# Output weights of FFN and experts loaded as neighbouring row pairs, with the inner FFN columns taken at a stride of two

## The reference

```python
def swiglu(h, w_in, w_out):
    g, u = jnp.split(h @ w_in, 2, axis=-1)
    return (jax.nn.silu(g) * u) @ w_out
```

## Time and profile before

| | |
|---|---|
| time, median of three runs | 2223.34 us (2221.9 to 2224.48) |
| span of the profiled execution, first to last instruction | 2220.3 us |
| TensorE busy | 2011.6 us, 91% |
| VectorE busy | 1409.2 us, 63% |
| ScalarE busy | 1195.9 us, 54% |
| GpSimd busy | 564.5 us, 25% |
| granted TensorE clock, mean | 0.962 |
| read from memory | 512.10 MB, 231 GB/s over the span |

### The profile page before, as it was taken

One profiled execution on the slowest core, in us unless ns is written; L12 is line 12 of the kernel. 1 busy time (PEld: TensorE's weight loads), 2 busy tenths in 40 slices (PEclk: granted clock), 3 DMA queues, 4 the chain that ended last, 5 costly groups with the idle time before them and its releaser, 6 DMA issues. The chain is left out here.

```text
span 2220.3 us, 25094 instructions
## 1 busy us (share of the span) xinstructions
PE 2011.6 (91%) x8940; PEld 1560.7 (70%) x8941; DVE 1409.2 (63%) x1276; ACT 1195.9 (54%) x1018; POOL 564.5 (25%) x192
## 2 busy tenths in 40 slices
PE   4888779999999788869999999999999999999895
PEld 2556568667678675557877788787877878777784
DVE  5657432544433352457878778787877878787784
ACT  5442442433322334446767676676766767676573
POOL 1310011211210110013324233333333423243232
PEclk9999889999999889989999999999999999999998
DMA  9560212545622221228989899898998979898792
GB/s 347 204 213 20 76 57 95 166 166 179 208 95 72 80 95 39 67 83 306 364 287 365 299 349 356 301 363 295 367 336 312 371 285 361 300 353 324 248 367 85
DMA packets 231745, 513.84 MB, mean 231 GB/s; under 512 B 9129, under 2 KB 34706, under 8 KB 231186
## 3 DMA queue, kind: packets, MB, share of 16 engines
q1 hardware_dynamic: 228498, 507.25, 64.2%
q10 hardware_dynamic: 3200, 5.96, 0.8%
HBM read 512.10 MB, written 1.07 MB: 231 GB/s over the span
## 5 line engine op out<-in xcount | busy, mean ns | idle before, releaser
L170 DVE TENSOR_TENSOR low<-raw,high 128x2048 fp32r<-128x2048 f32 (+2 forms) x484 | 1023.7, 2140 | 404.1 <-ACT high L162 397.3
L162 ACT ACTIVATE high<-raw 128x2048 fp32r<-128x2048 f32 (+1 forms) x484 | 923.7, 1912 | 623.5 <-PE PS L191 491.2
L170 POOL TENSOR_TENSOR low<-raw,high 128x1024 fp32r<-128x1024 f32 x161 | 527.1, 3274 | 1474.0 <-ACT high L162 1474.0
L189 PE MATMUL PS<-high,ah 128*128 128x512 f32 (+1 forms) x1478 | 592.0, 401 | 28.9 <-DVE low L170 12.9
L191 PE MATMUL PS<-high,al 128*128 128x512 f32 (+1 forms) x1478 | 577.5, 391 | 0.0
L190 PE MATMUL PS<-low,ah 128*128 128x512 f32 (+1 forms) x1478 | 577.2, 391 | 0.0
L189 PEld LDWEIGHTS PS<-high,ah 128*128 128x128 f32 x1478 | 280.6, 190 | 112.5 <-POOL low L170 28.0
L191 PEld LDWEIGHTS PS<-high,al 128*128 128x128 f32 x1478 | 280.4, 190 | 58.5
L190 PEld LDWEIGHTS PS<-low,ah 128*128 128x128 f32 x1478 | 281.0, 190 | 53.1
L1769 PE MATMUL PS<-high,ah 128*128 128x512 f32 x504 | 197.7, 392 | 4.0 <-DVE al L1343 4.0
L1771 PE MATMUL PS<-high,al 128*128 128x512 f32 x504 | 197.1, 391 | 0.0
(11 more groups left out here) (251 smaller groups left out, 1372.6 us busy)
## 6 DMA issues: line engine op xcount, KB each, us to landing
raw<-in_moe_w_in_dram SPq DMA_DIRECT2D x252, 1024.0 KB, 7.3
raw<-in_moe_w_out_dram SPq DMA_DIRECT2D x126, 1024.0 KB, 7.5
raw<-in_ada_w_dram SPq DMA_DIRECT2D x48, 1024.0 KB, 6.5
raw<-in_ffn_w_in_dram SPq DMA_DIRECT2D x22, 1024.0 KB, 5.1
raw<-in_ffn_w_out_dram SPq DMA_DIRECT2D x11, 1024.0 KB, 4.8
raw<-in_ab_w_in_dram SPq DMA_DIRECT2D x8, 1024.0 KB, 5.7
raw<-in_ab_w_out_dram SPq DMA_DIRECT2D x4, 1024.0 KB, 6.7
raw<-in_mla_w_o_dram SPq DMA_DIRECT2D x4, 1024.0 KB, 4.9
```

Of the source, the lines that this page charges most:

```text
L162: act.activation(high[n % SPL][:, 0:width], raw[n % RAW][:, 0:width], ACT.Copy).then_inc(high_made, 1)
L170: eng.tensor_tensor(low[n % SPL][:, c0:c1], raw[n % RAW][:, c0:c1], high[n % SPL][:, c0:c1].bitcast(F32), ALU.subtract).then_inc(low_made[ ...
L189: pe.matmul(o, sh, mh, start=start, stop=False)
```

## The change

`ffn_w_out` and `moe_w_out` are viewed by `row_pairs` instead: partition p of a unit holds rows 256u + 2p and 256u + 2p + 1, which lie next to each other in memory. Each partition thus reads one run of 8 KB where it read two runs of 4 KB. The bytes, the number of units and their order stay.

So that the rows of the hidden values match, block j of a pair in `ffn_pair` takes columns j, j+2, j+4, ... of its 256 instead of 128 neighbouring ones, and `turn` takes every second column of 256 of `hh`.

```diff
--- before.py
+++ after.py
@@ -583,8 +583,12 @@
         def rows_of(w):
             return w.rearrange("(k p) n -> p k n", p=P)
 
+        def row_pairs(w):
+
+            return w.rearrange("(u p a) n -> u p a n", p=P, a=2)
+
         abin, about = rows_of(ab_w_in[0]), rows_of(ab_w_out[0])
-        fin, fout = rows_of(ffn_w_in[0]), rows_of(ffn_w_out[0])
+        fin, fout = rows_of(ffn_w_in[0]), row_pairs(ffn_w_out[0])
         wdq, wdkv, wuq, wukv, wo = (rows_of(w[0]) for w in (mla_w_dq, mla_w_dkv, mla_w_uq, mla_w_ukv, mla_w_o))
 
         MLA_W = [4 * CQ] * 2 + [4 * (CKV + CROPE)] * 2 + [1536] * 3 + [2048] * 2 + [2048] * 4
@@ -665,28 +669,28 @@
             for j in range(2):
                 fin_pair(N_FIN + 42 + 2 * j, 0, (9 + j) * 256)
             for j in range(11):
-                load_unit(sp, N_FOUT + j, fout[:, 2 * j:2 * j + 2, :])
+                load_unit(sp, N_FOUT + j, fout[j])
             for j in range(13):
                 load_unit(sp, N_MLA + j, mla_src(j))
 
 
             def visit(v, e):
-                wi, wo_ = rows_of(moe_w_in[0, e]), rows_of(moe_w_out[0, e])
+                wi, wo_ = rows_of(moe_w_in[0, e]), row_pairs(moe_w_out[0, e])
 
                 def up(n, it, col):
                     for j in range(4):
                         load_unit(sp, n + j, wi[:, 4 * (j % 2):4 * (j % 2) + 4, bass.ds(col + (j // 2) * D_FFE, FCH)], it)
 
-                def down(n, it, blk):
+                def down(n, it, pair):
                     for j in range(2):
-                        load_unit(sp, n + j, wo_[:, bass.ds(blk + 2 * j, 2), :], it)
+                        load_unit(sp, n + j, wo_[bass.ds(pair + j, 1)].rearrange("u p a n -> p (u a) n"), it)
 
                 up(U0, v * NCH, 0)
                 with sp.Fori(0, 3) as i:
                     for j in range(2):
                         up(UC + 6 * j, v * NCH + i * 2, i * 1024 + (j + 1) * FCH)
-                        down(UC + 4 + 6 * j, v * NCH + i * 2, i * 8 + j * 4)
-                down(UC + 36, v * NCH, 24)
+                        down(UC + 4 + 6 * j, v * NCH + i * 2, i * 4 + j * 2)
+                down(UC + 36, v * NCH, 12)
 
             with sp.Fori(0, NE) as e:
                 visit(e, e)
@@ -1579,7 +1583,7 @@
                             unit_ready(pe, n + gu, it)
                         if gu == 0 and f >= 2:
                             pe.wait_ge(s["hid_made"], f - 1 + i * 4)
-                        wh, wl = (t[:, :, j * P:(j + 1) * P] for t in halves(n + gu, KD))
+                        wh, wl = (t.rearrange("p k (c a) -> p k c a", a=2)[:, :, :, j] for t in halves(n + gu, KD))
                         for k in range(KD):
                             if f == gu == 0:
                                 low_ready(pe, 1, k)
@@ -1740,7 +1744,8 @@
             def turn(count, par):
                 pe.wait_ge(s["h_made"], count)
                 for j in range(4):
-                    last = pe.transpose(PS[:, 4, j * P:(j + 1) * P], hh[:, par, j * P:(j + 1) * P], ident)
+                    last = pe.transpose(PS[:, 4, j * P:(j + 1) * P],
+                                        hh[:, par, :].rearrange("p (u c a) -> p u c a", c=P, a=2)[:, j // 2, :, j % 2], ident)
                 last.then_inc(s["ht_done"], 1)
 
             def up(n, it, par, parts=(0, 1)):
```

## The result

| | before | after |
|---|---|---|
| median, 11 runs each | 2224.26 us | 2230.6 us |
| ratio of after to before, 95% interval | | 1.003 (1.0018 to 1.0043) |
| span of the profiled execution | 2220.3 us | 2231.6 us |

The change makes the kernel slower by 0.3% (6.3 us between the medians), and the interval leaves no room for no change. The two profiled executions lie further apart, by 11.3 us; the next lines sort out why.

What follows compares the result with a forecast made beforehand. The prediction took TensorE's own instructions as the bound. Transfers, FFN loads and transposes gave 0 + 0 + 0 on a 2220.3 us span; 3.0 us from span to median made 2223.3 us, range 2217 to 2237 us.

Steps and rivals of the forecast that it cites:

- the transposes' bound: Experts' `turn`: 252 transposes with the loads' 53 ns column part doubled and exposed, 13.4 us, total 2237 us; 5 in 100.
- The rival of slower FFN loads: FFN's first product: strided loads cost by their span, up to 68 us, with transposes 81 us, 2305 us; 7 in 100.
- What bounds the kernel: Whole kernel: bound by TensorE's own instructions, busy 91% of the span; no transfer in the loop.
- The transfers, 0: FFN and expert output weights: 137 transfers in 8 KB runs, hidden behind TensorE's work, 3.5 us reserve; 0 us.
- transfers become the bound: Expert stage: 8 KB runs moving 20% slower would add 45 us over 63 chunks, 2268 us; 4 in 100.
- disturb the splits less: Expert stage: half as many runs might shorten GpSimd's splits, some 5 us back, 2218 us; 5 in 100.
- The strided transposes: Experts' `turn`: 252 strided transposes keep loads of 140 ns, taken as 0 us; upper bound 13.4 us.
- The strided loads of the FFN: `ffn_pair`, FFN's first product: 1056 loads at a stride of two floats, taken as 0 us; upper bound 68 us.
- 38 ns of each interval are free: FFN's first product: a load shown with 189 ns leaves 38 ns of the 0.227 us between matmul starts.
- the 0.23 us that was to show the prediction wrong: Sign in the FFN's trace: an interval between matmuls grown past 0.23 us means the prediction is wrong.
- The comparison by bytes per ns: FFN loads: strided span needs 10 bytes per ns, packed transpose loads read 9.7, bf16 some 23; so 0 us.
- The Trainium skill's rule on 16-byte lines: FFN's strided loads: full-rate reads need two accesses per 16-byte line; stride two has exactly two, so 0 us.

Runs made afterwards that it cites:

- e1: Against the kernel before, only `moe_w_out` is loaded in 8 KB runs, with TensorE's reads packed; 2224.59 us, ratio 1.0003.
- e11: Changed kernel, but ScalarE, VectorE and GpSimd sort the FFN's columns in the splits; 48 loads stay strided; 2221.86 us, ratio 1.0008 to before.
- e4: The change in the experts alone, the FFN as in the kernel before; 2222.65 us, ratio 0.9996.

## Why the prediction was wrong

Forecast was no change (2223.3 us, 0.79); slower had 0.16. The measured 2230.6 us is inside 2217 to 2237 but clear of no change. That it lies inside is luck: the upper end was the transposes' bound, and the transposes cost nothing that could be measured. The rival of slower FFN loads was to begin with a load 38 ns longer and reach 68 us; the load's row grew by 5 ns and the cost was 6.6 us.

- **What bounds the kernel:** right. TensorE's own pace sets the time. A loss of 6.6 us in its pace came through to the total (6.3 us between the medians).
- **The transfers, 0:** right. e1 shows 1.0003 (0.9994 to 1.0012) for the experts' runs, and e11 has all of them without the loss. ScalarE waited for no transfer; the rivals "transfers become the bound" and "disturb the splits less" both fall with it.
- **The strided transposes, 0 (bound 13.4 us):** right in time, wrong in the row, and so right by luck. The reason given was a reading rate in hand that would keep the loads at 140 ns, and they are 207. The bound assumed that a longer load delays its transpose by as much, and this fell: a round grew by 0.03 us, not by 4 x 0.053 = 0.21, and the ratio of e4 is 0.9996 (0.9988 to 1.0005).
- **The strided loads of the FFN, taken as 0 (bound 68 us):** this step failed. It measured 6.6 us. The wrong sentence is "38 ns of each interval are free", with its rule that "a load that is 30 ns longer costs nothing". It treated the shown 189 ns as the load's length. Measured by the pace, a packed load occupies 112 ns and a strided one 118. By either reading the loads fit, as I wrote, and the interval grew all the same, from 226.7 to 233.3 ns, past the 0.23 us that was to show the prediction wrong. So at 512 tokens a load which fits can cost something, though it cost nothing at 256 and 384. The comparison by bytes per ns foresaw no longer load; with 6 ns it was nearly right there, which didn't help.
- **The Trainium skill's rule on 16-byte lines:** the load went by it within 6 ns (112 packed, 118 at two floats to a line, 233 at one). The term of 0 that was taken from it for the sum was as wrong as mine, since it speaks of the read and not of the interval.

What stays open is why the interval, counted in cycles of 2.4 GHz, is the number of tokens plus 32 at 256, 384 and 512 packed tokens, but 16 more in most groups of 448 packed tokens and at 512 with strided loads. That the FFN's strided loads cause the loss is shown, by taking them out; how a load that fits lengthens the interval is not.

## What to carry to other kernels

Before making transfer runs longer, look whether anything waits for a transfer. Here ScalarE never did for these weights, and 17,536 fewer packets moved nothing. A layout that is free for the DMA can be paid for where the data is read: if the inner loop of the bounding engine reads it, let an engine with time to spare do the sorting, as in e11, or leave it. If a weight read like the FFN's must be strided, a stride of two floats cost less than four or eight (stages of 298.8, 301.3 and 310.7 us under 512 tokens, 305.4 and 534.0 under 256). Check the start-to-start interval in the trace, not the load's duration.

## What the runs showed that I had not expected

- A load's row is longer than the time for which it keeps the next load waiting: under 512 tokens, rows of 188, 193 and 310 ns stand for 112, 118 and 233 ns.
- Transposes' loads grow from 139 to 207 ns at a stride of two and stay at 208 at four, at no cost that the ratios resolve (a round takes 0.03 us more).
- A matmul of 448 tokens takes 206.7 ns, packed, in 41 of 44 groups and 202.7 in three, where 384 take 173.3 and 512 take 226.7.
- In one execution of the strided 448 + 64 cut the granted clock dropped to half 21 times in the FFN's stage, and that cost more than all strided loads did.
- SyncE's issue of a `moe_w_out` transfer went from 373 to 345 ns with the single run for each partition, without effect.
